# Token norms: the square root read from PSUM, its table loaded ahead, slot 1's low half after the tiles, two tiles built ahead

## What is computed

```python
def _rms_norm(x, g):
    xf = x.astype(jnp.float32)
    y = xf * lax.rsqrt(jnp.mean(xf * xf, axis=-1, keepdims=True) + NORM_EPS)
    return (y * g.astype(jnp.float32)).astype(x.dtype)
...
            h = _rms_norm(x, a_norm_g[j])
...
    proj = h @ w_in
...
def modulate(x, g, shift, scale):
    return rmsnorm(x, g) * (1 + scale) + shift

def swiglu(h, w_gu, w_down):
    gate, up = jnp.split(h @ w_gu, 2, axis=-1)
    return (jax.nn.silu(gate) * up) @ w_down
...
        h = modulate(x, norm1_g[layer], sh1, sc1)
...
        x = x + g2 * swiglu(modulate(x, norm2_g[layer], sh2, sc2), ffn_w_gu[layer], ffn_w_down[layer])
```

## Time and profile before

| | us |
|---|---|
| time before, median of 3 runs | 3489.56 (3489.02 to 3490.71) |
| the profiled execution's own time | 3496.51 |
| its span | 3494.7 |
| TensorE busy | 3192.0 (91% of the span) |
| VectorE busy | 1876.4 (54%) |
| ScalarE busy | 1124.4 (32%) |

### The profile page before, as it was taken

The page is one execution under the profiler, slowest core; times in us unless marked ns, Lnnn a source line. Parts: engine busy times, 40 slices in busy tenths (PEclk is TensorE's granted clock), DMA queues, the critical chain, the costliest instruction groups (busy, mean ns, idle before and its releaser), DMA issues. The chain is left out here.

```text
span 3494.7 us, 39262 instructions
## 1 busy us (share of the span) xinstructions
PE 3192.0 (91%) x15464; PEld 2504.9 (72%) x15464; DVE 1876.4 (54%) x2778; ACT 1124.4 (32%) x2065; POOL 133.2 (4%) x154
## 2 busy tenths in 40 slices
PE   6998897998899888898999888899999789989997
PEld 4876664666678653497888557688888667767875
DVE  4647698544663866614243898445253555442333
ACT  3346323355332822322122222321212144532221
POOL 0000000100100000001000120000000100000000
PEclk9999999999999999899999999999999899999999
DMA  4223212211321421221111215124142411122221
GB/s 147 85 61 134 78 59 85 85 48 38 138 96 59 127 103 72 85 76 46 61 60 42 89 61 181 73 90 139 60 151 84 150 57 30 65 74 95 96 90 55
DMA packets 57151, 299.18 MB, mean 86 GB/s; under 512 B 8375, under 2 KB 8631, under 8 KB 31080
## 3 DMA queue, kind: packets, MB, share of 16 engines
q1 hardware_dynamic: 46744, 259.90, 21.0%
q0 software_dynamic: 10256, 37.23, 3.3%
HBM read 269.05 MB, written 15.73 MB: 81 GB/s over the span
## 5 line engine op out<-in xcount | busy, mean ns | idle before, releaser
L410 PE MATMUL bank<-high,slot_high 128*128 128x512 f32 (+1 forms) x3344 | 1240.5, 371 | 137.2 <-DVE low L334 78.3
L411 PE MATMUL bank<-low,slot_high 128*128 128x512 f32 (+1 forms) x3344 | 1228.2, 367 | 0.0
L412 PE MATMUL bank<-high,slot_low 128*128 128x512 f32 (+1 forms) x3344 | 1225.2, 366 | 0.0
L390 DVE TENSOR_TENSOR slot_low<-slot,slot_high 128x2048 fp32r<-128x2048 f32 (+1 forms) x172 | 390.3, 2270 | 979.3 <-ACT slot_high L384 979.2
L410 PEld LDWEIGHTS bank<-high,slot_high 128*128 128x128 f32 x3344 | 636.2, 190 | 273.5 <-issue 120.7
L384 ACT ACTIVATE slot_high<-slot 128x2048 fp32r<-128x2048 f32 (+1 forms) x172 | 325.4, 1893 | 1364.4 <-PE bank L412 1171.2
L411 PEld LDWEIGHTS bank<-low,slot_high 128*128 128x128 f32 x3344 | 638.3, 191 | 109.8 <-issue 4.5
L412 PEld LDWEIGHTS bank<-high,slot_low 128*128 128x128 f32 x3344 | 635.8, 190 | 108.8
L1093 DVE TENSOR_REDUCE least<-bank 128x1 f32<-128x128 f32 (+2 forms) x224 | 105.2, 504 | 131.8 <-PE bank L3408 51.8
L1144 ACT ACTIVATE prob<-bank,least 128x128 f32<-128x128 f32 (+2 forms) x224 | 121.2, 555 | 36.9 <-DVE least L1097 29.9
L449 PE MATMUL bank<-slot_high,low 128*128 128x256 f32 x448 | 125.7, 280 | 0.0
(11 more groups left out here) (382 smaller groups left out, 3809.2 us busy)
## 6 DMA issues: line engine op xcount, KB each, us to landing
slot<-in_gu SPq DMA_DIRECT2D x44, 1024.0 KB, 4.7
slot<-in_a_in SPq DMA_DIRECT2D x32, 1024.0 KB, 4.8
whole<-in_mod POOLq DMA_DIRECT2D x56, 512.0 KB, 3.6
slot<-in_e_rest SPq DMA_DIRECT2D x16, 1024.0 KB, 4.8
slot<-in_down SPq DMA_DIRECT2D x16, 1024.0 KB, 4.8
spectra<-f_spectrum SPq DMA_DIRECT2D x12, 1024.0 KB, 3.8
h_spectrum<-spectra SPq DMA_DIRECT2D x12, 1024.0 KB, 5.0
mod_raw<-in_mod SPq DMA_DIRECT2D x22, 512.0 KB, 5.5
```

Of the source, the lines that this page charges most:

```text
L390: dve.tensor_tensor(k.slot_low[s][:, 0:n], k.slot[s][:, 0:n], k.slot_high[s][:, 0:n].bitcast(F32), ALU.subtract).then_inc(k.low[s], 1)
L410: pe.matmul(out, wh, xh, start=kt == 0, stop=False)
L411: pe.matmul(out, wh, xl, start=False, stop=False)
L412: mm = pe.matmul(out, wl, xh, start=False, stop=kt == self.kt - 1)
```

## The change

- A new instruction `warm_root`: ScalarE takes the root of one constant column (epsilon) into a scratch tile. It is put ahead of the squares: in `square` before the first, and in `TailSquares` before the first square of the tail. The table load goes with it.
- VectorE's copy of the mean (L668) is gone. ScalarE takes the root straight from PSUM, with epsilon as the bias, and waits for the bank to be filled. VectorE's reciprocal waits for the bank to be drained. The semaphore `root_ready` is gone at these places.
- In norms that are neither `summed` nor `given` (the first a, the first feed-forward part, the odd layer), slot 1's low part (L390) moves from before the tiles to behind them all, where it already stood in the others.
- `Feed` builds two tiles ahead, not three: b0 b1 l0 b2 b3 l1 b4 l2 and so on. This holds for all feeds, also those of the output projections.
- In the even layer's filter the first transform waits for the two banks' drain.

```diff
@@ class K
+    def warm_root(self, act):
+        act.activation(self.warm[:, self.warmed:self.warmed + 1], self.c("eps", 1), ACT.Sqrt)
+        self.warmed += 1
@@ Feed.vector
-        for y in range(3):
+        for y in range(2):
             build(y)
...
             ins.then_inc(low.sem, 1)
+            if y == 0:
+                build(2)
             build(y + 3)
@@ SplitNorm
     def square(self, k, act):
+        k.warm_root(act)
...
     def take_roots(self, k, act, u):
-        root = k.named("root_ready")
         for r, (c, n) in enumerate(self.ranges):
-            act.wait_ge(k.drained[7 - r], self.full(u, r))
-            act.activation(k.root[:, c:c + n], k.rstd[:, c:c + n], ACT.Sqrt).then_inc(root.sem, 1)
+            act.wait_ge(k.filled[7 - r], self.full(u, r))
+            act.activation(k.root[:, c:c + n], k.ps[7 - r][:, 0:n], ACT.Sqrt, bias=k.c("eps", 1)).then_inc(k.drained[7 - r], 1)
...
     def vector(self, k, dve, u):
         self.k, self.dve = k, dve
-        if not self.given:
-            self.take_means(k, dve, u)
         halve_first(k, dve, u, "take_low", self.phase, 0)
         if not self.given:
-            self.invert(k, dve)
-        if not (self.summed or self.given):
-            halve_first(k, dve, u, "take_low", self.phase, 1)
+            self.invert(k, dve, u)
         self.feed.vector(k, dve)
-        if self.summed or self.given:
-            halve_first(k, dve, u, "take_low", self.phase, 1)
+        halve_first(k, dve, u, "take_low", self.phase, 1)
...
-    def invert(self, k, dve):
-        root, inverse = k.named("root_ready"), k.named("rstd_ready")
+    def invert(self, k, dve, u):
+        inverse = k.named("rstd_ready")
         for r, (c, n) in enumerate(self.ranges):
-            dve.wait_ge(root.sem, root.at(r + 1))
+            dve.wait_ge(k.drained[7 - r], self.full(u, r))
             dve.reciprocal(k.rstd[:, c:c + n], k.root[:, c:c + n]).then_inc(inverse.sem, 1)
@@ TailSquares.scalar
                 b, f = p.bank(s, t), 4 * i + 2 * s + t
+                if f == 0:
+                    k.warm_root(act)
                 act.wait_ge(k.drained[b], u.full(b, i))
```

More of the change, by code:

```diff
@@ L53 @@
 CON, CON_COLS = layout([("ones", P), ("mean", P), ("ident", P), ("rot64", P), ("rot128", P), ("one_row", 31 + P),
-                        ("four_rows", 12 + P), ("two_rows", 4 + P), ("inv_n", 1), ("length", 2)])
+                        ("four_rows", 12 + P), ("two_rows", 4 + P), ("inv_n", 1), ("eps", 1), ("length", 2)])
 class Signal:
@@ L122, in __init__ @@
         self.rstd = self.sb("rstd", TOK)
+        self.warm, self.warmed = self.sb("warm", 16), 0
         self.ps = [ctx.enter_context(nc.psum_tensor(f"bank{b}", [P, BANK], F32)) for b in range(8)]
@@ L652, in vector @@
         self.k, self.dve = k, dve
-        if not self.given:
-            self.take_means(k, dve, u)
         halve_first(k, dve, u, "take_low", self.phase, 0)
         if not self.given:
-            self.invert(k, dve)
-        if not (self.summed or self.given):
-            halve_first(k, dve, u, "take_low", self.phase, 1)
+            self.invert(k, dve, u)
         self.feed.vector(k, dve)
-        if self.summed or self.given:
-            halve_first(k, dve, u, "take_low", self.phase, 1)
+        halve_first(k, dve, u, "take_low", self.phase, 1)
         u.add(self.banks())
-    def take_means(self, k, dve, u):
+    def invert(self, k, dve, u):
+        inverse = k.named("rstd_ready")
         for r, (c, n) in enumerate(self.ranges):
-            dve.wait_ge(k.filled[7 - r], self.full(u, r))
-            dve.tensor_scalar(k.rstd[:, c:c + n], k.ps[7 - r][:, 0:n], EPS, None, ALU.add)\
-               .then_inc(k.drained[7 - r], 1)
-    def invert(self, k, dve):
-        root, inverse = k.named("root_ready"), k.named("rstd_ready")
-        for r, (c, n) in enumerate(self.ranges):
-            dve.wait_ge(root.sem, root.at(r + 1))
+            dve.wait_ge(k.drained[7 - r], self.full(u, r))
             dve.reciprocal(k.rstd[:, c:c + n], k.root[:, c:c + n]).then_inc(inverse.sem, 1)
@@ L684, in counts @@
         n, r = len(self.order), len(self.ranges)
-        return dict(**self.feed.counts(), **({} if self.given else dict(root_ready=r, rstd_ready=r)),
+        return dict(**self.feed.counts(), **({} if self.given else dict(rstd_ready=r)),
                     **({} if self.summed or self.given else dict(squares=n, square_added=n - r)))
@@ L728, in counts @@
         n, r = len(self.order), len(self.ranges)
-        return dict(root_ready=r, rstd_ready=r, squares=n, square_added=n - r)
+        return dict(rstd_ready=r, squares=n, square_added=n - r)
 class Ring:
@@ L2932, in transform @@
                 pe.wait_ge(taps_in.sem, taps_in.at(2 * tap_at[x + 1]))
+                if x == 0:
+                    for b in (7, 6):
+                        pe.wait_ge(k.drained[b], u[0].full(b))
                 for f in range(H):
@@ L2981, in _ @@
                 dve.tensor_scalar(angle[0:64, :], angle[0:64, :], PI, -PI, ALU.min, ALU.max).then_inc(turns.sem, 1)
-            stats.take_means(k, dve, u[1])
             dve.wait_ge(tables_in.sem, tables_in.at(80))
@@ L3049, in _ @@
                     gains(k, dve, gain, 0, 0, (0, 1))
-                    stats.invert(k, dve)
+                    stats.invert(k, dve, u[1])
             dve.wait_ge(k.filled[3], u[1].full(3, 2))
@@ L3811, in constants @@
     put("inv_n", rows)
+    put("eps", np.full((P, 1), EPS))
     put("length", np.tile(np.array([[LAT, CTX]]), (P, 1)))
```

## The result

The change made the kernel a little slower: 3493.64 us (median of 13 runs, 3489.91 to 3503.95) against 3489.02 of before (13 runs beside them). The ratio is 1.0023, 95% interval 1.0016 to 1.0031, so 5.6 to 10.8 us slower. The two medians alone are 4.6 us apart, so the size is less certain than the sign. The prediction was 3482.4, faster. The profiled execution took 3493.47 us, its span 3491.7. One thing has to be kept in mind with two single executions: the profiled one of before (3496.51) was slow for that kernel, so the two spans, 3494.7 and 3491.7, say nothing on the sign.

What follows compares the result with a forecast made beforehand. Bound: TensorE's waits at the feeds' starts, behind a chain over ScalarE and VectorE. −3.4 − 3.4 − 1.2 − 1.9 + 0.5 + 0.5 = −8.9, with the clock −7.2: 3489.56 to 3482.4 us; range 3477.0 to 3487.0.

Steps and rivals of the forecast that it cites:

- Parts b, c and the second feed-forward part: Starts of these three: load and copy gone −1.29, bias +0.05, feed stall +0.12; −1.12 each, −3.4 in all.
- Second a: Its start: the copy's 0.67 and the root's 0.67 go, −1.34, feed stall +0.12; −1.2.
- First a: Its start: reciprocal earlier −1.5, slot 1's low part moved −2.24, small root 0.20, feed stall 0.12; −3.4.
- First feed-forward part and odd layer: Their starts: bare load +1.48, copy −0.72, bias +0.05, slot 1's low part −2.25, stall +0.47; −0.97 each, −1.9 together.
- The clock: Odd layer's sums: TensorE's longer pause, 3.4, makes the clock fall there too, +1.7; upper bound +5.1, lowest −1.7.
- two tiles ahead in the feeds of sixteen: VectorE stalls ahead of the first low part: +0.47 in first feed-forward part and odd layer, +0.5 in the even layer.
- rival 5: All thirteen feeds: uneven first tiles delay the full clock one stretch each, 22 us; slower, 3504.4; chance 0.05.
- Rival 1: Clock doesn't fall in the odd layer, 3480.7; first feed-forward part spared too, 3479.0; chance 0.28.
- Rivals 3 and 4: TensorE waits for slot 1's low part, 3489.1, chance 0.07; table loaded again ahead of the root, 3486.2, chance 0.05.

Runs made afterwards that it cites:

- e1: The kernel before with one unused tile of 64 bytes per partition where the change put its scratch tile: 3500.80 us, ratio 1.0038 to before.
- e3: The change as it is, run once more: 3492.48 us, ratio 1.0012 to the kernel before.
- e2: The whole change with its scratch column kept among the constants, so no tile lies elsewhere than before: 3482.76 us, ratio 0.9986 to before.
- e4: The kernel before, unchanged, profiled a second time; the runs of before in its group have a median of 3486.95 us.
- e15: e2 again (nothing shifted, two tiles ahead everywhere), on the same chip as e13 and e16: 3482.62 us, ratio 0.9982 to before.
- e16: e2 with three tiles built ahead in place of two: 3478.41 us, ratio 0.9970 to before.
- e13: e2 with two tiles ahead only in the ten feeds of eight tiles, three in those of sixteen: 3478.22 us, ratio 0.9971 to before.
- e9: The kernel before with two tiles built ahead in every feed as the only change, nothing shifted: 3493.73 us, ratio 1.0012 to before.
- e5: The kernel before with an unused tile of 32 bytes where e1 had 64: 3480.16 us in one execution.
- e6: The kernel before with an unused tile of 128 bytes where e1 had 64: 3492.91 us in one execution.
- e10: The kernel before with the weight slots moved 64 bytes down, the streamed tiles left where they were: 3496.66 us in one execution.

## Why the prediction was wrong

**The step that failed is one that isn't in it.** The part-by-part account takes the diff's instructions one by one and leaves out its allocation. `self.sb("warm", 16)` issues nothing, and so it got no term, no bound and no rival; not even the rival that ends slower has it. It cost 13 us (e1 by its times; 12.7 by the pace of its matmuls, and 12.4 in the change itself, e3 against e2), more than all that the steps gained.

**The steps that are in it held.** Without the shift the change gave −4.9 (−8.0 to −1.7) and −6.3 (−9.4 to −3.1), against −7.2. In detail, in the profile after:
- The starts as a whole: from the last matmul of the part before to the 49th of the feed, b and c took 21.99 us each against 23.10 in e4, the second feed-forward part 22.44 against 23.44, the second a 24.05 against 25.05. That is −1.1, −1.1, −1.0 and −1.0, where the prediction has −1.12 three times and −1.2. In the first a, from the first sum on, it is −3.2 (predicted −3.4, with the 0.2 of the small root, which stands ahead of the sums), in the odd layer, up to the feed's first matmul, 25.03 against 24.35, +0.7 (−0.97 + 1.69 predicted).
- Parts b, c and the second feed-forward part: root at the barrier, reciprocal 0.72 behind (0.67 + 0.05 predicted), first low part 1.45 behind the first build (1.46).
- Second a: the reciprocal starts right behind VectorE's other work, at 927.72, the root long done at 925.6. (That other work waits 4.32 for a DMA of `lam`, so it is this DMA that sets the start here.)
- First a: the low part of slot 0 starts at 24.19, ends last ahead of the reciprocal (26.40), the builds stand at 29.78. TensorE had no wait for slot 1's low part.
- First feed-forward part and odd layer: the load cost 1.40 (2792.46 to 2793.86, 1.48 predicted), the root from PSUM with the bias column 0.69 instead of 0.63, the stall 0.39 ahead of the first low part, so 1.54 from first build to first low part (1.53).
- The clock: the odd layer's sums took 12.25, as forecast; e15 and e16 show that they need not.

**Probably mis-sized: two tiles ahead in the feeds of sixteen.** The step has 1.4, VectorE's stall; e13 to e16 give 3.7, uncertain by 2. The stall itself is right (0.48 in the first feed-forward part). On top of it the clock took another 1.5 there in three of six profiles, though not in that of the change. The prediction had this as rival 5, for all feeds and at 0.05. For all thirteen feeds together 2.5 is inside what was measured (4.2 uncertain by 3; 0.7 to 7.7 in e9). It is not what made the forecast fail: e2 and e15 have two tiles ahead and are faster than before.

**The rivals.** Rival 1 (no fall of the clock in the odd layer) happened in two of ten profiles, not in that of the change. Rivals 3 and 4 did not happen: no second load stands ahead of a root, and slot 1's low part is off the path. The drain that the Trainium skill adds to a table load ("ScalarE: Activation LUTs", section "What ACT_TABLE_LOAD costs") isn't in the trace after either: the small root starts 0.02 behind the load's end (2793.74 and 2793.76).

**What could have been seen.** Not the amount: no row of before shows how the pace depends on the place. But the pace itself is there to be read. Two stretches of the kernel before, both of matmuls of 512 columns alone, the first at the end of the first a, the second in b:

```profile
321.50:361.50 40.00, 40.00 (x176) 1.00 0.31 106
380.00:420.00 40.00, 40.00 (x172) 1.00 0.29 105
```

Both run at the full clock without a break, and yet it is 176 in the one and 172 in the other, 0.227 and 0.233 us each. That difference of 2% says that something other than the instruction sets the pace. On TensorE's 3192.0 busy us, 2% are 64 us, an estimate of the size up to which a diff that moves operands could cost or give; measured were +12.7 (e1) and −7.3 (e5).

## What to carry to other kernels

An allocation is a part of a diff like an instruction: list which tiles move, and where TensorE streams without a break count its matmuls per stretch before and after, at the full clock. To judge an edit that needs a new tile, put the tile where nothing else moves (padding, the end of the stack), or run the kernel before with the same gap as a control. And a place can be chosen: 32 unused bytes ahead of two parts were worth about 8 us here, more than the whole rearrangement without its gap (5 to 6, e2 and e15).

## What the hardware showed that was not expected

- The pace of back-to-back matmuls at the full clock depends on where the streamed operand and the weights lie in on-chip memory: with the streamed operand moved by 32 (e5), 128 (e6), 0 (before) and 64 bytes (e1) the same six took 1.039, 1.046, 1.049 and 1.060 us, worked out from 2310, 2294, 2288 and 2265 or 2266 matmuls in 400 us. Moving the weights by 64 the other way gave 1.060 again (e10), which speaks for the distance between the two.
- Two executions of before differ by some 11 us, 1.1 of it in the pace of matmuls at the full clock; their mean granted clocks are 0.961 and 0.965.
